# One decoder step in split fp32 on one core: gate and up products by one level of Strassen's algorithm, FFN tiles in three parts

## What is computed

```python
x = x + 0.5 * ((silu(rms(x) @ w_gate1) * (rms(x) @ w_up1)) @ w_down1)   # half FFN 1, 1024 -> 2816 -> 1024
z = rms(x) @ w_in                       # [pool 512 | q 512 | k 128 | v 128]
x = x + concat(pool(z), attn(z)) @ w_out
x = x + 0.5 * ((silu(rms(x) @ w_gate2) * (rms(x) @ w_up2)) @ w_down2)   # half FFN 2
```

## Time and profile before

| | |
|---|---|
| time of 3 runs | 965.12 us median (965.09 to 965.76) |
| time of the profiled execution | 965.15 us |
| its span, first to last instruction | 963.4 us |
| PE busy | 943.8 us, 98% |
| DVE busy | 425.2 us, 44% |
| ACT busy | 274.0 us, 28% |
| POOL busy | 99.7 us, 10% |
| HBM traffic | 90 GB/s over the span |

### The profile page before, as it was taken

How to read it: one execution, slowest core, us unless ns; L and a number is a source line. 1 busy time by engine, 2 the same in 40 slices (tenths; PEclk the granted TensorE clock), 3 DMA queues, 4 the chain that set the end, 5 groups by cost and what they waited for, 6 DMA issues and landing times.

```text
span 963.4 us, 18000 instructions
## 1 busy us (share of the span) xinstructions
PE 943.8 (98%) x7556; PEld 920.8 (96%) x7556; DVE 425.2 (44%) x527; ACT 274.0 (28%) x382; POOL 99.7 (10%) x78
## 2 busy tenths in 40 slices
PE   5999999999999999999998999999999999999998
PEld 4999999999999999999865899999999999999998
DVE  7444444444443434343775575444444444322221
ACT  5322222222222122133455324223222232211110
POOL 4000000000002212133212451000000000000000
PEclk9999999999999999999999999999999999999999
DMA  6222222222332222152300122222223223333310
GB/s 236 88 87 87 87 87 87 90 90 89 108 108 91 90 90 73 45 178 83 111 23 22 57 87 89 96 100 87 87 88 102 93 87 103 120 106 107 112 41 22
DMA packets 24791, 87.57 MB, mean 91 GB/s; under 512 B 3232, under 2 KB 3616, under 8 KB 24768
## 3 DMA queue, kind: packets, MB, share of 16 engines
q1 hardware_dynamic: 23008, 84.45, 26.7%
q10 hardware_dynamic: 1760, 2.81, 0.8%
HBM read 83.31 MB, written 3.60 MB: 90 GB/s over the span
## 4 chain that ended last, share of the span: by engine, by line
PE 95%; DVE 3%; issue 1%; POOL 0%; DMA 0%; ACT 0%; POOLq 0%; DVEq 0%
PE ps L409 90%; PE ps L592 1%; PE ps L613 1%; DVE xlo L951 1%; PE ps L604 0%; DMA fixed<-fixed 0%; PE ps L427 0%; PE ps L589 0%; PE ps L515 0%; DVE wlo L945 0%; DVE small L1118 0%; POOL sqsum L1270 0%; PE ps L434 0%; PE ps L644 0%; PE ps L624 0%
## 5 line engine op out<-in xcount | busy, mean ns | idle before, releaser
L409 PE MATMUL ps<-xhi,whi 128*128 128x268 f32 (+1 forms) x1568 | 321.8, 286 | 11.0 <-DVE xlo L951 11.0
L726 ACT CAST whi<-raw 128x1024 fp32r<-128x1024 f32 (+1 forms) x138 | 155.3, 1125 | 618.5 <-PE ps L409 615.7
L409 PE MATMUL ps<-xlo,whi 128*128 128x268 f32 (+1 forms) x1568 | 319.0, 285 | 0.0
L409 PE MATMUL ps<-xhi,wlo 128*128 128x268 f32 (+1 forms) x1568 | 317.9, 284 | 0.0
L409 PEld LDWEIGHTS ps<-xhi,whi 128*128 128x128 f32 x1568 | 242.8, 189 | 15.3 <-issue 12.3
L945 DVE TENSOR_TENSOR wlo<-raw,whi 128x1024 fp32r<-128x1024 f32 (+1 forms) x138 | 194.1, 1406 | 127.6 <-ACT whi L726 127.6
L409 PEld LDWEIGHTS ps<-xhi,wlo 128*128 128x128 f32 x1568 | 243.5, 189 | 0.0
L409 PEld LDWEIGHTS ps<-xlo,whi 128*128 128x128 f32 x1568 | 243.4, 189 | 0.0
L409 PE MATMUL ps<-hhi,wlo 128*128 128x268 f32 (+1 forms) x704 | 143.0, 285 | 0.0
L409 PE MATMUL ps<-hlo,whi 128*128 128x268 f32 (+1 forms) x704 | 142.9, 284 | 0.0
L409 PE MATMUL ps<-hhi,whi 128*128 128x268 f32 (+1 forms) x704 | 142.6, 284 | 0.0
(11 more groups left out here) (142 smaller groups left out, 486.8 us busy)
## 6 DMA issues: line engine op xcount, KB each, us to landing
raw<-gu SPq DMA_DIRECT2D x88, 512.0 KB, 3.3
raw<-d SPq DMA_DIRECT2D x32, 704.0 KB, 3.9
raw<-w_in SPq DMA_DIRECT2D x10, 512.0 KB, 3.6
raw<-w_out SPq DMA_DIRECT2D x8, 512.0 KB, 4.0
xT<-x SPq DMA_DIRECT2D x8, 268.0 KB, 5.2
o_y<-ybuf ACTq DMA_DIRECT2D x8, 260.0 KB, 2.1
ckT<-ck SPq DMA_DIRECT2D x1, 512.0 KB, 5.1
cv<-cv SPq DMA_DIRECT2D x1, 512.0 KB, 5.7
```

Source lines behind the costliest of these rows:

```text
L409: last = nc.tensor.matmul(dst[:, s, 0:n], w[:, c % 2, kk, :], x[:, k, c0 + s * n:c0 + (s + 1) * n], start=(k == 0 and w is whi and x is hi ...
L726: nc.scalar.copy(whi[:, c % 2, 0:t, :], raw[:, c % RAW, 0:t, :]).then_inc(whi_ready, 1)
```

## The change

**Products.** For FFN tile f the weights of gate and up, [1024 x 128] each, are seen as a 2x2 matrix of blocks (the halves of the model dimension by gate or up), and the activations as a 2x2 matrix (the halves of the model dimension by the halves of the token columns). One level of Strassen's algorithm in Winograd's form makes the four sums with 7 products of 4 blocks instead of 8. Each product takes 12 matmuls (4 block pairs `pr`, 3 split terms), one after the other into one bank. The first 4 tiles of FFN 1 and the first tile of FFN 2 stay as before ("plain"); the other 18 and 21 are the Strassen units.

```diff
+        def unit_product(s, p, i, name):
+            n = STAGES[s]["n"]
+            block, slot = PROD[name]
+            dst = (chain_bank(s, p, i, n) if name in ("P1", "P6", "P5", "P3") else
+                   pair_bank(s, p, i, n) if name in ("P7", "P4") else single_bank(n))
+            first = name in ("P1", "P7", "P2")
+            for pr in range(KC):
...
+                nc.tensor.matmul(dst, whi_t, xhi_t, start=(first and pr == 0), stop=False, skip_group_check=True)
+                nc.tensor.matmul(dst, whi_t, xlo_t, start=False, stop=False, skip_group_check=True)
+                last = nc.tensor.matmul(dst, wlo_t, xhi_t, start=False, stop=(pr == KC - 1), skip_group_check=True)
+            last.then_inc(products, 1)
...
+            for i in range(1, n):
+                p1(s, p, i)
+                p7(s, p, i)
+                p3(s, p, i - 1)
+                p6(s, p, i)
+                p4(s, p, i - 1)
+                p2(s, p, i)
+                p5(s, p, i)
+            down(s, p, 0, [0])
+            p3(s, p, n - 1)
+            p4(s, p, n - 1)
+            down(s, p, 0, list(range(1, TILES[p])))
```

```diff
+        def weight_sums(s, p, i):
...
+            nc.vector.tensor_tensor(full[:, r, 1:5:3, :], full[:, r, 1:5:3, :], full[:, r, 0:7:6, :], ALU.add
+                                    ).then_inc(added, 1)
+            dve.wait_ge(added, u + 1)
+            nc.vector.tensor_tensor(full[:, r, 2, :], full[:, r, 1, :], full[:, r, 6, :], ALU.add
+                                    ).then_inc(s2_made, 1)
+            dve.wait_ge(s2_made, u + 1)
+            nc.vector.tensor_tensor(full[:, r, 5, :], full[:, r, 2, :], full[:, r, 3, :], ALU.add
+                                    ).then_inc(s4_made, 1)
```

More of the change, by code:

```diff
@@ L370, in _ @@
             sp.dma_start(dst, src).then_inc(mixin_loaded, 16)
[L371 to L372 removed]
+        for m in range(IN_UNITS):
+            load(U_IN + m, a["w_in"], m * KD * P)
         load(U_OUT, a["w_out"], 0)
@@ new lines, in warm_up, with early @@
+        def warm_up():
+            pe.wait_ge(zeros_made, 1)
+            for _ in range(WARM):
+                nc.tensor.matmul(nsum[:, 0, 0:2 * P], hid[:, 0:P], hid[:, 0:2 * P], start=True, stop=True)
+        def early(c, dst, pairs, n, wait, first=False, last=False):
+            x = x_split(n)
+            for k in range(KD):
+                for i, (w, lo) in enumerate(pairs):
+                    wait(k, i)
+                    for h in range(2):
+                        done = nc.tensor.matmul(dst[:, h, 0:n], w[:, c % 2, chunk(k), :], x(k, lo, h),
+                                                start=(first and k == 0 and i == 0),
+                                                stop=(last and k == KD - 1 and i == len(pairs) - 1))
+            if last:
+                done.then_inc(unit_done, 1)
@@ new lines, in part @@
+        def part(s, p):
+            n = PARTS[s][p]
+            p1(s, p, 0)
+            p7(s, p, 0)
+            p6(s, p, 0)
+            p2(s, p, 0)
+            p5(s, p, 0)
+            for i in range(1, n):
[10 more added lines that the diff above has]
+            down(s, p, 0, list(range(1, TILES[p])))
+            for d in range(1, KD):
+                down(s, p, d)
@@ L482, in project @@
+        plain_products_1()
+        for p in range(3):
+            part(0, p)
         def project(m, ks=None, wait_k=None):
@@ L706, in _ @@
         out_product(1, [3, 4, 5, 6, 7])
-        with pe.Fori(0, KD // 2 - 1) as it:
-            out_product(2, it=it)
-            out_product(3, it=it)
-        ffn_products(STAGES[1], True)
+        for d in range(2, KD):
+            out_product(d)
+        plain_products_2()
+        for p in range(3):
+            part(1, p)
     @block.scalar
@@ new lines, in keep_u4, with silu_0 @@
+        def keep_u4(s, p, i):
+            u, n = unit_no(s, p, i), STAGES[s]["n"]
+            act.wait_ge(products, product_no(s, p, i, "P5"))
+            if u:
+                act.wait_ge(up1_taken, u)
+            nc.scalar.copy(u4c[:, 0:n], chain_bank(s, p, i, n)).then_inc(u4_kept, 1)
+        def silu_0(s, p, i):
+            u, n, c0 = unit_no(s, p, i), STAGES[s]["n"], STAGES[s]["c0"]
+            act.wait_ge(gate0_scaled, u + 1)
+            if i:
+                act.wait_ge(hid_made, u)
+            nc.scalar.activation(act_gate[:, c0:c0 + n], gate[:, c0:c0 + n], ACT.Silu).then_inc(silu0_ready, 1)
@@ new lines, in scale_gate0 @@
+        def scale_gate0(s, p, i):
+            u, n, c0 = unit_no(s, p, i), STAGES[s]["n"], STAGES[s]["c0"]
+            cols = slice(c0, c0 + n)
+            dve.wait_ge(products, product_no(s, p, i, "P2"))
+            dve.wait_ge(p1_kept, u + 1)
+            if i:
+                dve.wait_ge(silu0_ready, u)
+            elif 3 * s + p:
+                dve.wait_ge(x_added, KD * (3 * s + p))
+            nc.vector.tensor_tensor(gate[:, cols], single_bank(n), p1c[:, 0:n], ALU.add).then_inc(c11_summed, 1)
+            dve.wait_ge(c11_summed, u + 1)
+            nc.vector.tensor_tensor(gate[:, cols], gate[:, cols], rstd[:, cols], ALU.mult).then_inc(gate0_scaled, 1)
@@ L1047, in _ @@
+        plain_hid(0, 2, pair[1])
+        split_lo(7)
+        hid_lo(0, 2, 2)
+        t_sums(0, 3, 0, 0, n)
+        t_lo(0, 3, n)
+        weight_sums(0, 0, 0)
+        weight_lo(0, 0, 0, 0)
+        plain_gate(0, 3, pair[0])
+        weight_lo(0, 0, 0, 1)
+        weight_lo(0, 0, 0, 2)
+        plain_hid(0, 3, pair[1])
+        hid_lo(0, 3, 3)
+        for p in range(3):
+            part(0, p)
         invert(2, nrm[:, 1, 0:BLKS], nrm[:, 0, 0:BLKS])
@@ L1286, in _ @@
         pool.wait_ge(sqsum_zero, 1)
-        with pool.Fori(0, KD) as it:
-            square(0, E_B1, 0, NH_ALL, 1, it)
+        for d in range(KD):
+            square(d, 1, 0, NH_ALL, x_added, KD * 2 + d + 1)
         pool.wait_ge(unit_done, U_IN)
@@ L1359, in _ @@
         pool.wait_ge(sqsum_zero, 2)
-        with pool.Fori(0, KD) as it:
-            square(0, E_OUT, META, NH_OUT, 2, it)
+        for d in range(KD):
+            square(d, 2, META, NH_OUT, evacuated, E_OUT + d + 1)
     ctx.close()
```

965 lines of the change are left out of this document (682 added, 283 removed).

## The result

The changed kernel takes 929.41 us median (928.55 to 930.73, 4 runs), beside 965.44 us (965.09 to 966.33, 4 runs) for the kernel before: ratio 0.9627, 95% interval [0.961, 0.9643]. That is 36.0 us off, where the prediction had 40.5. The profiled execution took 930.73 us, 34.4 less than the one of before.

What follows compares the result with a forecast made beforehand. TensorE, busy 98% of the span, was taken as the bound: -56.7 (saved matmuls) + 1 + 5.5 - 5.7 + 3.2 + 1.5 + 0.75 + 10 = -40.5 us against 965.15, so 925 us; own range 916 to 936, wider range 910 to 946.

Steps and rivals of the forecast that it cites:

- start: Kernel start: with GpSimd's squares gone, `x_lo` gets shorter and the third unit with the norm comes earlier, -5.7 us.
- plain tiles: wait: Plain tiles of FFN 1: the seventh unit's weight split ends at 49.5, TensorE wants it at 46.3, +3.2 us (0 to 6).
- end of FFN 1, norm and mixer: End of FFN 1: two more operations behind the last down product, later GpSimd square, norm waits about 1.5 us.
- w_out, two waits: w_out steps: split weights come late for w_out unit 7 and the first FFN 2 unit, 1.6 + 1.85 us.
- norm and spread ahead of FFN 2: Behind w_out: TensorE waits 4.8 us for the last summed square, then 1.9 for the root behind `t_hi` and a table load.
- the price of 0: Strassen products: matmuls summing on in one bank cost no more than alternating ones; taken as 0, bounds 0 to 46 us.
- rival (c): Strassen products: a matmul summing in its neighbour's bank costs more; with 14 ns each the time is 971 us; chance 0.05.
- rival (a): Strassen rounds: VectorE and ScalarE set the pace, 10.8 us a round, +24 us less the 1 charged: 948 us; chance 0.15.
- FFN 2's is on the edge: FFN 2's Strassen rounds: VectorE's second split ends at S + 14.6, P3 is due at S + 14.5.
- rival (b): w_out steps and plain tiles: VectorE catches up, so no 10 and no 3.2 us: 912 us; chance 0.11.
- `keep_u4` waits: Ends of the six parts: P3 of the last unit waits 0.55 us for ScalarE's copy, six times, 3.3 us.
- rival (d): Small missed waits, in transfers or in the mixer with its three `raw` slots: 940 us; chance 0.09.

Runs made afterwards that it cites:

- run 6: Changed kernel plus a needless VectorE addition of 536 columns in each of the 33 rounds that are not the first of a part: 940.76 us.
- run 1: Changed kernel with the w_out steps' squares moved from GpSimd to ScalarE and summed by VectorE: 925.62 us.
- run 2: Changed kernel with the sums and splits of FFN 2's first Strassen unit moved from the w_out steps to behind the last one: 925.48 us.
- run 3: Changed kernel with the third pair's activation sums in FFN 1's plain tiles moved behind the weight splits of plain units 7 and 8: 926.58 us.
- run 4: Changed kernel plus 26 needless fp32 matmuls placed ahead of five long TensorE waits: 927.04 us.
- run 10: Run 8 plus an idle time of TensorE of about 4 us ahead of four parts (seven GpSimd clearings each): 944.82 us.
- run 11: Run 8 plus an idle time of TensorE of about 1.8 us ahead of four parts (three GpSimd clearings each): 925.15 us.
- run 7: Changed kernel with two token tiles instead of one in the first down block ahead of P3 at the end of each part: 927.32 us.
- run 8: Changed kernel with the edits of run 2, run 3 and run 7 together: 916.34 us.
- run 9: Run 8 with w_out's squares and FFN 1's last square on ScalarE, and the last pair's `t_hi` behind the norm's root: 910.29 us.

## Why the prediction came out as it did

It said 925 us in a range of 910 to 946, and 929.4 came. By its own steps, in the profiled executions (positions of the same matmul in both traces; a wait is counted as the distance of starts less 0.12):

| step | predicted | measured |
|---|---|---|
| FFN 1 behind the first Strassen start (products, ends, beginnings) | -23.9 | -24.15 |
| FFN 2 behind the plain tile | -26.2 | -26.1 |
| start | -5.7 | -5.8 |
| plain tiles: wait | +3.2 | +4.2 |
| end of FFN 1, norm and mixer | +1.5 | +3.5 |
| w_out, two waits | +3.45 | +3.95 |
| norm and spread ahead of FFN 2 | +6.7 | +6.8 |
| tail | +0.75 | +0.7 |
| clock behind the plain tiles' wait | none | +2.4 |

The right-hand column gives -34.5 us, against 34.4 between the two executions. The left-hand one gives -40.2, the prediction's own -40.5 up to rounding (it took 10 for 10.15).

The nearness of the number is not luck in the main: apart from the clock the steps agree with the traces to about 1 us each, and the miss of 4.4 us (6.1 in the profiled executions) is mostly one missing term, below.

**What held.** A chain of fp32r matmuls in one bank costs 123.0 and 119.7 ns against the 123.75 and 119.0 of the earlier trace rows: the price of 0 was right, the 14 ns of the earlier trace rows do not carry over to this chain, and rival (c) is out. The rounds are TensorE's, rival (a)'s 10.8 us did not come, and the step that decided between them, 0.09 us of overlap between VectorE operations in the earlier trace rows, was borne out by run 6: VectorE's list is 10.10 and 10.03 us. By the rule that the prediction quoted from the Trainium skill (VectorE: DVE Perf Modes, The TRN2 errata), taken without overlap, it would be 10.42 and TensorE would have waited; run 6 decides against that reading by 0.3 us. "FFN 2's is on the edge" was literally right, by 0.02 us. The 9.56 us summed for VectorE were short of the 10.0 to 10.1 measured, and so the margin of FFN 1 was thinner than said. Rival (b) is out as well: the waits in w_out and the plain tiles came, and runs 1, 2 and 3 removed them.

**What failed.** The step "Sum" has no term for the clock. The prediction counts each wait of TensorE at its own length (3.2, 4.8 and 1.9 us), though the earlier trace rows gives the prices of matmuls at full clock only. Behind the waits of the changed kernel matmuls ran at 1.2 GHz for 3.4 or 6.8 us each time. Counted by starts that is 6.7 us in four places. Paid are 2.4 behind the plain tiles' wait, 1.6 at the end of FFN 1, 0.3 at the norm ahead of FFN 2, and 1.1 in the attention beyond what the kernel before pays there: 5.4 us, most of the 6.1 by which the two profiled executions miss the -40.5. Runs 4, 10 and 11 show the clock as a cause and not a companion: with it held up the kernel is faster though it does more, and idle times of 4.6 us cost about 1.5 us a piece beyond themselves, those of 2.2 us nothing.

**What looks wrong and is not.** The norm's wait was 3.76 us instead of 4.8, and the spread's 0.4 instead of 1.9. That is again the clock: the slow matmuls took the place of waiting. Without them the waits are 5.3 us (run 7) and 1.4 (runs 4 and 8), together the 6.7 predicted. So this row is right for the reason given, each of its two terms to 0.5 us.

**What was mis-sized.** "Gate of the third tile is scaled at 46.5 ... end at 49.5" was a microsecond early: that gate was scaled at 47.5, and VectorE's split ended at 50.4. At the end of FFN 1 the wait was 1.8 us instead of 1.5, and the clock fell behind it. What else separates the two kernels from there through the attention is the clock too, and not the mixer with its three `raw` slots, which rival (d) named: run 9, with the same three slots but neither that wait nor the low clock, takes 116.3 us from the last down matmul of FFN 1 to the first w_out matmul, and the kernel before 116.7. Of the six `keep_u4` waits 0.4 us stand as a bracket, 0.41 to 0.52 in the distance of starts, where 0.55 was said; run 7 took them away.
